# Expert weights loaded as whole 2 MB matrices into neighbouring slots, in place of 1 MB halves

## The reference, cut to what matters

```
pg = softmax(h @ w_rg + b_rg);  p_grp, g_sel = top_k(pg, 1)            # 4 groups
pe = softmax(logits of the 8 experts of that group)
top_p, top_i = top_k(pe, 2)                                            # 2 experts for each row
def expert(xblk, e):                                                   # 32 experts, blocks of 128 rows
    return (silu(xblk @ w_eg[e]) * (xblk @ w_eu[e])) @ w_ed[e]
y = sum over the two experts of a row of gate * expert output
```

## Time and profile before

| | |
|---|---|
| median of 3 runs | 991.25 us (991.07 to 991.28) |
| profiled execution | 992.78 us, its span 990.9 us |
| PE busy | 945.9 us (95%) |
| DVE busy | 840.9 us (85%) |
| ACT busy | 586.6 us (59%) |
| weight loads | 64 of w_eg, 64 of w_eu, 64 of w_ed, 1024 KB each; median 8.5, 9.5 and 9.9 us from issue to landing |
| all DMA | 275.72 MB, mean 278 GB/s over the span |

### The profile page before, as it was taken

How to read it: one execution, slowest core, us unless ns; L and a number is a source line. 1 busy time by engine, 2 the same in 40 slices (tenths; PEclk the granted TensorE clock), 3 DMA queues, 4 the chain that set the end, 5 groups by cost and what they waited for, 6 DMA issues and landing times.

```text
span 990.9 us, 14018 instructions
## 1 busy us (share of the span) xinstructions
PE 945.9 (95%) x4771; PEld 801.5 (81%) x4771; DVE 840.9 (85%) x978; ACT 586.6 (59%) x564; POOL 168.4 (17%) x201
## 2 busy tenths in 40 slices
PE   5999999999999989999999999999999999999973
PEld 5999978987888777788888888888888888888751
DVE  6488998988687697999898998989989899898857
ACT  7311111574532144888777887778877788777514
POOL 1000000000000021632231222312223122231210
PEclk9999999999999979999999999999999999999997
DMA  9321251314332846899999999999999999999988
GB/s 286 118 65 43 67 154 58 112 34 161 128 128 86 329 130 222 335 403 378 401 370 389 378 379 392 384 385 391 387 403 379 397 392 380 397 389 384 340 267 311
DMA packets 68028, 275.72 MB, mean 278 GB/s; under 512 B 12783, under 2 KB 27631, under 8 KB 43417
## 3 DMA queue, kind: packets, MB, share of 16 engines
q1 hardware_dynamic: 56281, 255.97, 68.7%
q0 software_dynamic: 9792, 17.85, 4.7%
q10 hardware_dynamic: 1920, 1.44, 0.6%
HBM read 259.34 MB, written 31.38 MB: 293 GB/s over the span
## 4 chain that ended last, share of the span: by engine, by line
PE 57%; DVE 4%; DMA 2%; ACT 1%; issue 1%; SPq 0%; POOLq 0%; POOL 0%; DVEq 0%; ACTq 0%
PE ps L1234 11%; PE ps L1236 11%; PE ps L1235 11%; PE ps L1253 6%; PE ps L1251 6%; PE ps L1252 6%; PE ps L1206 3%; DVE big L1808 2%; PE ps L1260 1%; DMA y_scratch<-arena,cur 1%; ACT arena L947 1%; DMA arena<-y_scratch 1%; DVE arena L1905 0%; PE ps L1347 0%; PE ps L1190 0%
## 5 line engine op out<-in xcount | busy, mean ns | idle before, releaser
L1808 DVE TENSOR_TENSOR big<-arena,big 128x2048 fp32r<-128x2048 f32 x128 | 286.9, 2283 | 0.0
L843 ACT ACTIVATE big<-arena 128x2048 fp32r<-128x2048 f32 x128 | 238.8, 1910 | 3.5 <-DMA arena<-in_w_eg 1.8
L1234 PE MATMUL ps<-big,ring 128*128 128x512 f32 x508 | 201.1, 396 | 3.2 <-DVE big L1808 3.2
L1236 PE MATMUL ps<-big,ring 128*128 128x512 f32 x508 | 198.0, 390 | 0.0
L1235 PE MATMUL ps<-big,ring 128*128 128x512 f32 x508 | 197.6, 389 | 0.0
L1808 DVE TENSOR_TENSOR slot_tail<-arena,slot_tail 128x2048 fp32r<-128x2048 f32 x62 | 138.9, 2281 | 0.0
L843 ACT ACTIVATE slot_tail<-arena 128x2048 fp32r<-128x2048 f32 x62 | 115.5, 1918 | 0.2 <-DVE eob L1784 0.2
L1234 PEld LDWEIGHTS ps<-big,ring 128*128 128x128 f32 x508 | 95.4, 188 | 22.6 <-DVE big L1808 4.0
L1236 PEld LDWEIGHTS ps<-big,ring 128*128 128x128 f32 x508 | 95.3, 188 | 20.3
L1235 PEld LDWEIGHTS ps<-big,ring 128*128 128x128 f32 x508 | 95.5, 188 | 18.7
L1251 PE MATMUL ps<-slot_tail,hTr 128*128 128x512 f32 x248 | 99.2, 400 | 0.0
(11 more groups left out here) (280 smaller groups left out, 1485.3 us busy)
## 6 DMA issues: line engine op xcount, KB each, us to landing
arena<-in_w_eg SPq DMA_DIRECT2D x64, 1024.0 KB, 8.5
arena<-in_w_eu SPq DMA_DIRECT2D x64, 1024.0 KB, 9.5
arena<-in_w_ed SPq DMA_DIRECT2D x64, 1024.0 KB, 9.9
arena<-in_x_prompt SPq DMA_DIRECT2D x16, 512.0 KB, 5.1
arena<-y_scratch SPq DMA_DIRECT2D x16, 512.0 KB, 8.8
arena<-in_w_in SPq DMA_DIRECT2D x12, 512.0 KB, 4.0
arena<-in_conv_band SPq DMA_DIRECT2D x8, 576.0 KB, 4.3
arena<-in_w_out SPq DMA_DIRECT2D x8, 512.0 KB, 4.1
```

What stands on the lines that cost most here:

```text
L843: act.activation(we_h[n % SLOTS], raw[n % RAWS], ACT.Copy).then_inc(high_done, 1)
L1234: pe.matmul(out, part_h[b][:, k, :], wh[:, i, :], start=(k == 0), stop=False)
L1236: ins = pe.matmul(out, part_l[b][:, k, :], wh[:, i, :], start=False, stop=(k == KD - 1))
L1808: dve.tensor_tensor(we_l[n % SLOTS], raw[n % RAWS], we_h[n % SLOTS].bitcast(F32), ALU.subtract).then_inc(low_done, 1)
```

## The change

A matrix's two halves are neighbours in memory, in each partition's row of 4096 floats, and the raw slots are neighbours in the arena. The changed kernel loads a matrix by one transfer of 128 partitions x 4096 floats into the slots n and n + 1. SP waits until both slots are free. The six semaphores raw_in become three, one for two slots; ACT waits for the semaphore of the slot pair ahead of either half, so the first half is cast when the whole matrix has landed. Casts, subtractions, matmuls and their orders stay as they are, on pieces of 2048 floats. A pair has six weight transfers in place of twelve. The last load and the overflow loop are changed alike.

```diff
-        raw_in = [sem(f"raw_in{s}") for s in range(RAWS)]
+        raw_in = [sem(f"raw_in{s}") for s in range(RAWS // 2)]
...
-            def load_piece(n, piece, e):
-                b, m, half = piece
+            def load_matrix(n, piece, e):
+                b, m, _ = piece
                 w = {"g": w_eg, "u": w_eu, "d": w_ed}[m]
                 src = w[0, bass.ds(e[b], 1), :, :].rearrange("a (p k) n -> p (a k n)", p=P)
-                sp.dma_start(raw[n % RAWS], src[:, half * HP:(half + 1) * HP]).then_inc(raw_in[n % RAWS], 16)
+                s = n % RAWS
+                sp.dma_start(arena[:, s * HP:(s + 2) * HP], src).then_inc(raw_in[s // 2], 16)
...
-            def weights(j, pieces=range(NP)):
+            def weights(j, pieces=range(0, NP, 2)):
                 e = {-1: j - 1 + E // 2, 0: j, 1: j + E // 2}
                 for n in pieces:
-                    slot_free(sp, low_done, j, n)
-                    load_piece(n, PIECES[n], e)
+                    slot_free(sp, low_done, j, n + 1)
+                    load_matrix(n, PIECES[n], e)
...
-                    weights(0, (0, 1, 2, 3, 10, 11))
+                    weights(0, (0, 2, 10))
...
-                for n in range(NP):
-                    sp.wait_ge(low_done, over_free(j, n))
-                    load_piece(n, OVER_PIECES[n], e)
-
-            weights(0, (6, 7, 8, 9))
+                for n in range(0, NP, 2):
+                    sp.wait_ge(low_done, over_free(j, n + 1))
+                    load_matrix(n, OVER_PIECES[n], e)
+
+            weights(0, (6, 8))
             pair_loop(sp, weights, 1)
-            for s, n in LAST.items():
-                sp.wait_ge(low_done, after(PAIRS - 1, s + RAWS))
-                load_piece(s, PIECES[n], {-1: E - 1})
+            sp.wait_ge(low_done, after(PAIRS - 1, 1 + RAWS))
+            load_matrix(0, PIECES[LAST[0]], {-1: E - 1})
...
-                act.wait_ge(raw_in[n % RAWS], raw_count(j, n))
+                act.wait_ge(raw_in[n % RAWS // 2], raw_count(j, n))
...
             for s in LAST:
-                act.wait_ge(raw_in[s], 16 * (2 * PAIRS + 1))
+                act.wait_ge(raw_in[s // 2], 16 * (2 * PAIRS + 1))
```

More of the change, by code:

```diff
@@ L900, in over_high @@
             def over_high(j, n):
-                act.wait_ge(raw_in[n % RAWS], over_raw(j, n))
+                act.wait_ge(raw_in[n % RAWS // 2], over_raw(j, n))
                 act.wait_ge(piece_used, over_free(j, n))
```

## The result

The changed kernel takes 1010.47 us (median of 4 runs), the kernel before, in alternation with it, 991.26 (4 runs). By these medians it is slower by 19 us. Its runs spread more than those of the kernel before: 1002.87, 1007.52, 1013.42 and 1021.36 us against 991.07 to 992.52.

What follows compares the result with a forecast made beforehand. PE was taken to bound the expert loop at 17.69 us a half-round. Loop 0, start +0.3, removed issues 0 and end 0 took the profiled 992.78 to 993.1 us, median 991.5; range 990.0 to 1000.0.

Steps and rivals of the forecast that it cites:

- same: Whole kernel: time stays within 2 us of the 991.25 us median; chance 0.64.
- the load loop takes PE's place: Expert loop, first rival: F + 9.3 exceeds PE's 17.69 us, over 0.2% slower, 1000.5 to 1009 us; chance 0.30.
- F + 9.3: Expert loop: least half-round, F plus 3.72 us of casts plus 5.58 to the next issue; F's limit 8.4 us.
- F: Pieces 0/1 and 6/7: time from a whole matrix's issue to its landing, taken as 8.0 us, bounded by 6.1 and 9.1.
- the 0 us for the other four matrices: Pieces 2/3, 4/5 and their likes: first half issued about 2.2 us later, absorbed by ACT's short waits; 0 us.
- sign named for the first rival: Profile after: PE waits for L1808 or L1820, DVE waits for ACT ahead of L1813, half-round is F + 9.3.
- the prediction's own price: Expert loop: loss of (F - 8.4) x 28 - 2.0 us above the limit; 0 at the F taken.
- the buffer of 2.0 us: Expert loop: lateness that may gather over the whole loop before PE waits, about 2.0 us.
- The 9.1 us of two pieces: Loop start: (1,7) and (1,8), issued at 409.9 and 411.9 into a queue taken as empty; high end of F.
- the start: Where the expert loop starts: 0.3 us added, from the issue at 409.9 us; pair 0's matrices said not to matter.
- The loop steadies itself: Argument against the first rival: a longer half-round gives the DMA more time for the same bytes.
- The removed issues, the packets and the end: Six fewer issues a pair (0.33 us of SP each), perhaps half the weight packets, last matrix and scatter: each 0 us.

Runs made afterwards that it cites:

- e5: Kernel before, both halves issued when the second slot is free and cast only when both have landed, still two 1 MB transfers: 1015.74 us, 1.0223.
- e3: Changed kernel with the matrices of pieces 0/1 and 6/7 again loaded in halves, the other four whole: 991.72 us, 1.0001.
- e4: Kernel before with only the matrices of pieces 0/1 and 6/7 loaded whole: 1006.08 us, 1.0133.
- e8: Changed kernel with gather indices out of bounds from the third block on, so those gathers bring no rows: 995.23 us, 1.0043.
- e6: Changed kernel with DVE doing low 1 (and 7) right behind low 0 (6), ahead of rows_low and hidden: 997.12 us, 1.0059.
- e1: Kernel before, either half issued only when the second slot is free, ACT still waiting for each half by itself: 997.16 us, 1.0061.
- after_again: The changed kernel run a second time, source of the second profile: 1009.04 us, 1.0112; profiled execution 1008.76 us.

## Why the prediction was wrong

**The forecast was 991.5 us, 0.64 for "same"; the rival "the load loop takes PE's place" (0.30) is what happened.** The time of 1010.5 lies beyond the range's 1000.0.

*The mechanism and the limit were right.* "A half-round can't be shorter than F + 9.3" held: the difference was 9.2 to 9.4 us in 28 rounds of the profile after, and in e5's as well. So did the place (pieces 0/1 and 6/7), which e3 and e4 show from both sides, and the 0 us for the other four matrices, by e3's 1.0001. Each sign named for the first rival came: PE waits for L1821, DVE for ACT's cast ahead of low 0, and the round is F + 9.3.

*The step that failed is the size of F.* It was taken as 8.0 us; it is 9.15 on average. By the prediction's own price, (9.15 - 8.4) x 28 - 2.0 = 19.0 us for the profiled execution, and the loop grew by 21.1. The second profile gives, by the row of its first and last w_eg issue above, F = (886.3 - 453.0) / 24 - 9.3 = 8.75. The price says 7.8; the loop grew by 12.7. Part of the gap is a round of 20.3 us ahead of 440 us, which that mean leaves out: the 28 rounds from 414.8 us on take 506.7 us, and 506.7 - 28 x 17.69 = 11.4. The rest is less than the buffer of 2.0 us. A loop that begins 4.9 us late may have used it up before; that wasn't tested.

*Why F was mis-sized.* The argument was that on the DMA engines that come last there is no gap between the old work and the new, so that F is what the second half takes today, 7.7 us. That was no odd piece: second halves take 7.8 us on average in the profile before. But what comes last in the changed kernel takes 9.2 us, by the increments shown with e8, and it is there that the step fails. The rival put the delay on the engines that were ahead and start from nothing. That alone isn't enough for it: the first and the middle increments come in time, at 6.9 and 7.4 us, and e8's last at 7.8. What makes the last ones late are in the main the gathered rows, which the prediction didn't reckon with. Why they cost a whole matrix more than they cost the second half in the kernel before isn't shown.

The gap behind the issue is there, but it is not new. In the profile after, columns as in the earlier trace rows:

```profile
614.80:616.80 2.00, 2.00 (x13) 1.67 (x12) 2.00 (x2) 2.00 (x2) 0.00 (x0) 1.00 0.91 385
616.80:618.80 2.00, 2.00 (x10) 1.66 (x9) 2.00 (x2) 1.99 (x3) 0.33 (x1) 1.00 0.77 270
618.80:620.80 2.00, 2.00 (x10) 1.65 (x10) 2.00 (x1) 1.03 (x1) 1.18 (x2) 1.00 1.04 408
```

The DMA engines have a share of 0.77 in the 2 us behind the issue. The kernel before has 279 GB/s in the microsecond of the earlier trace rows and in the next:

```profile
604.00:605.00 1.00, 1.00 (x6) 0.83 (x5) 1.00 (x2) 1.00 (x2) 0.78 (x1) 1.00 0.88 279
```

New is what stands behind the gap: a whole matrix, where before the first half was already on its way.

*The number that stood for it.* The 9.1 us of two pieces were kept as the upper bound and set aside, because the queue isn't empty in the steady loop; they were nearly F itself (9.15 and 8.75). Rows 10 were misread: the queue wasn't empty there either. Piece (1,6), issued at 405.65 us in that profile, took 7.4 us and landed at 413.0, 3.1 us behind the issue of (1,7). So the 9.1 us were taken in a state like the loop's. A piece without other weights under way was in the trace too: (1,0), issued at 383.86, took 5.0 us, so 6.1 wasn't the low end. In the changed kernel the matrix (1,0), issued at 395.73 us with no other weights under way, takes 8.7. That the rival's 1009 for an F of 9.1 comes within 1.5 us of the median is partly luck, since all of its 17.6 us stood in the loop and none at the start.

*"The loop steadies itself" was right, but stops too late.* Longer rounds go with a shorter F: F was 10.8 us in e6, 10.4 in e1 with rounds of 17.83, and 9.15 in the changed kernel. But its round settled at 18.45 us, not at 17.69.

*A second step: the start.* It was priced at 0.3 us, with a bound of 0.5 on PE, from the issue at 409.9 us alone. "The matrices of pair 0 are loaded some 25 us ahead of their use and don't matter" is where it failed: they don't, but the gather of the second block's rows goes beside them, and what waits for it starts 3.0 us later. With the clock and the late weights behind it that is 4.9 to 7.0 us in the two profiles.

*The removed issues, the packets and the end* were put at 0, and nothing speaks against it. The rule of the Trainium skill, "SBUF — State Buffer", section "The DMA setup-cost knee", that the prediction weighed asks for the largest transfer one can have. No run here shows a gain over the kernel before from it, with 2048 KB for all matrices or for four of six; where it changes the waits, it costs 1.6%.

## What to carry to other kernels

A transfer that fills two slots waits for the later of them and is used only when all of it has landed. Before joining two, find the pair whose slots come free furthest apart in the consumer's order, write down the loop from landing to next issue, and compare it plus the time of the whole transfer with the round. Don't take today's time of the second half for it (7.7 us here; the matrices then took 7.7 to 10.5): the last of 16 shares counts, and other traffic lengthens that one. A matrix with no weights ahead of it, 8.7 us, was nearer. Then test the two waits with the old transfers (e5): that is an edit of two lines. And look at what shares the DMA with the transfers in the prologue, a gather on another queue above all.

## What was not expected of the hardware

A small gather on one queue is held up by how the other queue's transfers are made. It lands at 377.9 us with 2 MB matrices under way, at 375.7 with the same matrices as two transfers each (e5); the issues lie within 0.3 us. The other profiles agree: 377.6 to 378.1 us with both matrices whole (`after_again`, e6, e8), 376.9 with one of the two whole (e4), 375.5 with neither (e1). Which of the two does it, the larger packets or the whole 2 MB being queued at once, was not taken apart. The Trainium skill has a rule that would fit the packets: "DMA: Bandwidth & Descriptors", section "Queues, rings and completion order", says that each engine takes turns between queues a packet at a time. No run here shows that by itself.

A wait of 2.6 us on PE was followed by a granted clock of 0.54 over the next 6 us in the profile after and 0.65 in the second profile of the same kernel. After waits of 2.2 us in e6 and 2.5 us in e8 at the same place it stayed at 1.00; what decides between them isn't shown. e6's row:

```profile
378.00:384.00 6.00, 6.00 (x40) 5.47 (x41) 1.52 (x3) 3.26 (x3) 0.00 (x0) 1.00 0.10 40
```
